# Two-map attention: value products in three rounded passes over pairs of query tiles

## What is computed

```python
def diff_attention(q, k, v, pos, slopes, lam):
    scale = A_HEAD_DIM ** -0.5
    ...
    s = jnp.einsum('bqhmd,bkhmd->bhmqk', qb, k).astype(jnp.float32) * scale
    ...
    s = s - slopes[None, :, None, None, None] * dist
    p = jax.nn.softmax(s, axis=-1)
    w = p[:, :, 0] - lam * p[:, :, 1]
    return jnp.einsum('bhqk,bkhe->bqhe', w.astype(v.dtype), v)
```

## Time and profile before

| what | us |
|---|---|
| runs | 3290.07, 3291.96, 3292.62; median 3291.96 |
| profiled execution: its own time | 3290.69 |
| its span | 3288.9 |
| PE busy / DVE busy / ACT busy / POOL busy | 3188.6 / 1707.1 / 1131.5 / 997.7 |
| window 1467.40 to 1547.35, one head: PE / DVE / ACT / POOL busy | 79.95 / 52.93 / 43.02 / 17.50 |
| window 1867.00 to 1947.00, last head and after: PE / DVE / ACT / POOL busy | 80.00 / 44.60 / 46.65 / 25.23 |

### The profile page before, as it was taken

How to read it: one execution, slowest core, us unless ns; L and a number is a source line. 1 busy time by engine, 2 the same in 40 slices (tenths; PEclk the granted TensorE clock), 3 DMA queues, 4 the chain that set the end, 5 groups by cost and what they waited for, 6 DMA issues and landing times.

```text
span 3288.9 us, 52109 instructions
## 1 busy us (share of the span) xinstructions
PE 3188.6 (97%) x20350; PEld 2839.4 (86%) x20350; DVE 1707.1 (52%) x2867; ACT 1131.5 (34%) x2189; POOL 997.7 (30%) x688
## 2 busy tenths in 40 slices
PE   8999999999999999999999999999999999799997
PEld 6677768788888888999899899999999999699997
DVE  5554556765554535666666632277677033522223
ACT  3433333333332214555555541166465111300002
POOL 3112224787773333222222132210000223022222
PEclk9999999999999999999999999999999999799998
DMA  4011112122225112000000012211111341478888
GB/s 160 26 33 33 33 65 103 64 77 78 77 82 207 52 45 98 20 20 20 20 21 26 14 43 79 74 43 48 38 45 50 129 156 51 181 257 315 307 315 291
DMA packets 94214, 312.01 MB, mean 95 GB/s; under 512 B 14690, under 2 KB 27810, under 8 KB 90832
## 3 DMA queue, kind: packets, MB, share of 16 engines
q1 hardware_dynamic: 68448, 248.16, 21.3%
q10 hardware_dynamic: 19424, 42.70, 3.4%
q0 software_dynamic: 6160, 18.63, 2.3%
HBM read 247.91 MB, written 56.22 MB: 92 GB/s over the span
## 4 chain that ended last, share of the span: by engine, by line
PE 54%; DVE 3%; DMA 1%; ACT 1%; issue 1%; POOL 0%; SPq 0%; ACTq 0%; POOLq 0%; DVEq 0%
PE PS L673 14%; PE PS L3162 7%; PE PS L3631 6%; PE PS L661 5%; PE PS L3226 4%; PE PS L3378 4%; PE PS L3193 3%; PE PS L3661 3%; PE PS L3412 3%; PE PS L3454 2%; DVE EB L2837 1%; PE PS L3227 0%; DMA fin<-h_rows 0%; PE PS L3175 0%; DMA h_rows<-y_row_b,pick_s_b 0%
## 5 line engine op out<-in xcount | busy, mean ns | idle before, releaser
L695 POOL CAST w_hi<-ring 128x1024 fp32r<-128x1024 f32 x130 | 138.1, 1062 | 1543.9 <-PE PS L673 401.4
L697 POOL TENSOR_TENSOR w_lo<-ring,w_hi 128x1024 fp32r<-128x1024 f32 x130 | 333.4, 2565 | 10.5
L2247 ACT ACTIVATE EA<-EA,small_sb 128x1040 f32<-128x1040 f32 x144 | 166.6, 1157 | 186.4 <-DVE small_sb L2690 186.3
L2690 DVE CUSTOM_DVE_ANT_0 EA<-PS,biasH,low_a 128x1024 f32<-128x1024 f32 x128 | 163.6, 1278 | 56.3 <-PE PS L3193 56.2
L3162 PE MATMUL PS<-u_hi,w_hi 128*128 128x348 f32 x504 | 173.5, 344 | 0.0
L3162 PE MATMUL PS<-u_lo,w_hi 128*128 128x348 f32 x504 | 162.1, 322 | 0.0
L3162 PE MATMUL PS<-u_hi,w_lo 128*128 128x348 f32 x504 | 161.8, 321 | 0.0
L1643 DVE TENSOR_TENSOR hid_lo<-hid,hid_hi 128x1024 fp32r<-128x1024 f32 x44 | 91.7, 2123 | 118.8 <-ACT hid_hi L1285 118.8
L1735 PE MATMUL PS<-u_hi,w_hi 128*128 128x512 f32 x352 | 146.8, 417 | 3.0 <-POOL w_lo L697 2.3
L1932 PE MATMUL PS<-t_hi,slot_hi 128*128 128x512 f32 x352 | 138.9, 395 | 5.9 <-DVE t_lo L1544 3.3
L3226 PE MATMUL PS<-Va,PTa 128*128 128x128 f32 (+1 forms) x1152 | 139.9, 275 | 0.0
(11 more groups left out here) (502 smaller groups left out, 8639.5 us busy)
## 6 DMA issues: line engine op xcount, KB each, us to landing
ring<-in_stream SPq DMA_DIRECT2D x130, 512.0 KB, 3.5
w_gate_sb<-in_w_gate SPq DMA_DIRECT2D x64, 512.0 KB, 6.8
w_up_sb<-in_w_up SPq DMA_DIRECT2D x64, 512.0 KB, 8.1
w_down_sb<-in_w_down SPq DMA_DIRECT2D x64, 512.0 KB
gu_raw<-in_gate_up SPq DMA_DIRECT2D x22, 1024.0 KB, 5.6
hid_keep<-hid_out SPq DMA_DIRECT2D x17, 512.0 KB, 2.9
hid<-hid_keep ACTq DMA_DIRECT2D x15, 512.0 KB, 16.4
x_keep<-xT ACTq DMA_DIRECT2D x1, 4176.0 KB, 13.8
```

The costliest lines, as they stand in the source:

```text
L695: pool.tensor_copy(w_hi[j][:, :, :], w_raw[j][:, :, :]).then_inc(S["w_rounded"], 1)
L697: pool.tensor_tensor(w_lo[j][:, :, :], w_raw[j][:, :, :], w_hi[j][:, :, :], ALU.subtract).then_inc(S["w_split"], 1)
L2247: act.activation(e[0:m, :], e[0:m, :], ACT.Exp, scale=-1.0, bias=small[0:m, 8 + 2 * par + k:9 + 2 * par + k], accum_out=small[0:m, 12 + 2 ...
L2690: dve.tensor_tensor_reduce(e[0:m, 0:T1], wide(2 * k, T1, m), bias, -1.0, low_a[0:m, t, k:k + 1], ALU.add, ALU.min, low).then_inc(S["aa_max ...
```

## The change

The value product is done for groups of tiles, (0,1), (2,3), (4,5), (6,7,8), with values stationary and probabilities moving (256 or 272 columns), in three passes of rounded operands; the results come out as columns, are copied to SBUF and turned back with transposes. ACT writes the turned probabilities rounded (PA_hi) in two copies of 512 columns and one for the meta rows; DVE writes the rest (PA_lo). The same holds for the values. Four of the nine tiles of o_tok (t = 5 to 8, HELD = 5) no longer stay in SBUF: their results go to small staging tiles and by DMA to `o_keep` in DRAM, four DMAs a head on ACT's queue, and are loaded back after the last head.

```diff
+A_GROUPS = ((0, 1), (2, 3), (4, 5), (6, 7, 8))
+HELD = 5
...
 POOL
                 for t in range(NT + 1):
+                    if t == HELD:
+                        pool.wait_ge(S["keep_ld"], 32 + 16 * SPILLED)
                     heads_norm(pool, t).then_inc(S["as_np"], 1)
                 split(pool, FIRST_BRANCH, 1, MG0 // 2 + 2, FIRST_BRANCH - 2)
...
 ACT, for each step t of a head
+                        if t % 2 and before:
+                            results(*before)
                         if after:
                             exp(after[0], (after[1] + after[2]) % 2, after[2], 0)
+                        if t % 2 == 0 and before:
+                            take_columns(*before)
+                        if t % 2 or t == NT:
+                            take_pt(h, t)
                         if after:
                             exp(after[0], (after[1] + after[2]) % 2, after[2], 1)
+                        if t % 2 == 0 and t < NT:
+                            take_pt(h, t)
+                        if t % 2 and before:
+                            squares(*before)
...
 ACT, after the last head
+                take_columns(HEADS - 1, NGA - 1)
                 sigmoid(0, 0, EARLY_GATES[0], 0)
+                results(HEADS - 1, NGA - 1)
+                squares(HEADS - 1, NGA - 1)
                 roots(slice(HEADS - 1, HEADS))
+                act.wait_ge(S["keep_st"], KEPT + 16 * SPILLED * HEADS)
+                for t in range(HELD, NT + 1):
+                    m = P if t < NT else META
+                    act.dma_start(o_tok[0:m, t, :], o_keep[0:m, t - HELD, :]).then_inc(S["keep_ld"], 16)
...
 DVE
+                def attend(h, par, t, fresh=False, lower=None, first=False):
                     scores(h, par, t, 0, fresh)
                     scores(h, par, t, 1, fresh)
+                    if lower and first:
+                        lower_probs(*lower)
                     combine(h, par, t, fresh)
+                    if lower and not first:
+                        lower_probs(*lower)
...
-                            attend(h, (odd + t + 1) % 2, t + 1, first)
+                            attend(h, (odd + t + 1) % 2, t + 1, first, (h, t), t % 2 == 1)
...
 PE
+                def values(h, g, half):
+                    n, w = 9 * h + A_GROUPS[g][-1], group_width(g)
+                    pe.wait_ge(S["probs_lo"], 3 * n + 2 + half)
+                    if g == 0:
+                        pe.wait_ge(S["values_lo"], 3 * h + 2 + half)
+                    for i in (range(4, NT + 1) if half else range(4)):
+                        v_hi, v_lo = (Va_hi[:, i, :], Va_lo[:, i, :]) if i < NT else (Vam_hi[:, :], Vam_lo[:, :])
+                        for k, (v, probs) in enumerate(((v_hi, PA_hi), (v_hi, PA_lo), (v_lo, PA_hi))):
+                            last = mm(bank(7, w), v, probs[:, i, 0:w], start=(i == 0 and k == 0), stop=(i == NT and k == 2))
+                    if half:
+                        last.then_inc(S["aa_o"], 1)
+                def turn_back(h, g, n):
+                    pe.wait_ge(S["columns_in"], NGA * h + g + 1)
+                    pe.wait_ge(S["probs_lo"], 3 * n + 1)
+                    for k, t in enumerate(A_GROUPS[g]):
+                        m = P if t < NT else META
+                        last = turn(bank(7, P, k * P, m), turned_back[:, k * P:k * P + m])
+                    last.then_inc(S["aa_v"], 1)
...
 PE, for each step t of a head, after scores(t+1)
+                        before = None if first and t == 0 or t == NT or t % 2 else group_before(h, t)
+                        if before:
+                            values(*before, 1)
                         unit(h + 1, 1 - odd, kind, c, 0)
                         turn_probs(h, (odd + t) % 2, t, first)
                         unit(h + 1, 1 - odd, kind, c, 1)
+                        if t in (1, 3, 5, NT):
+                            values(h, min(t // 2, NGA - 1), 0)
+                        if before:
+                            turn_back(*before, 9 * h + t)
+                        if t == 0:
                             turn_values(h)
```

More of the change, by code:

```diff
@@ L348, in build @@
         ka_lo[1] = o.put("ka_lo1", [P, TP], F32R)
+        kmeta = o.put("kmeta", [P, 2 * META])
+        Vam_hi, Vam_lo = (o.put(n, [P, P], F32R) for n in ("Vam_hi", "Vam_lo"))
+        stage = [o.put("stage0", [P, P])]
         tok_at = (top - 4 * (NT + 1) * D) // 32 * 32
@@ new lines, in take_pt @@
+                    if cols.start == 0 and n:
+                        act.wait_ge(S["aa_o"], NGA * h + t // 2)
+                    act.activation(PA_hi[0:META, NT, cols], bank(7, m, 3 * P, META), ACT.Copy).then_inc(S["aa_pt"], 1)
+                    for b in range(2):
+                        act.wait_ge(S["aa_t"], 3 * n + 2 + b)
+                        act.activation(PA_hi[:, 4 * b:4 * b + 4, cols], bank(5 + b).rearrange("p (j n) -> p j n", n=P)[:, :, 0:m], ACT.Copy).then_inc(S["aa_pt"], 1)
@@ new lines, in take_columns, with home, results @@
+                def take_columns(h, g):
+                    w = group_width(g)
+                    act.wait_ge(S["aa_o"], NGA * h + g + 1)
+                    act.activation(turned_back[:, 0:w], bank(7, w), ACT.Copy).then_inc(S["columns_in"], 1)
+                def home(h, t, m):
+                    return o_tok[0:m, t, bass.ds(h * P, P)] if t < HELD else stage[t - HELD][0:m, :]
+                def results(h, g):
+                    act.wait_ge(S["aa_v"], TURNED_A * h + 4 + g)
+                    if g == NGA - 1 and h + 1 < HEADS:
+                        act.wait_ge(S["values_lo"], 3 * (h + 1) + 1)
+                    for k, t in enumerate(A_GROUPS[g]):
+                        m = P if t < NT else META
+                        if t == HELD:
+                            act.wait_ge(S["keep_st"], KEPT + 16 * SPILLED * h)
+                        seen(act)
+                        act.activation(home(h, t, m), bank(7, P, k * P, m), ACT.Copy, scale=small[0:m, 48 + t:49 + t]).then_inc(S["aa_y"], 1)
@@ new lines, in squares @@
+                def squares(h, g):
+                    for t in A_GROUPS[g]:
+                        m = P if t < NT else META
+                        act.wait_ge(S["aa_y"], 9 * h + t + 1 + CREDIT)
+                        if t >= HELD:
+                            act.dma_start(o_keep[0:m, t - HELD, h * P:(h + 1) * P], stage[t - HELD][0:m, :]).then_inc(S["keep_st"], 16)
+                        act.activation(junk[0:m, :], home(h, t, m), ACT.Square, accum_out=ss2[0:m, t, bass.ds(h, 1)]).then_inc(S["aa_ssq"], 1)
+                        act.wait_ge(S["aa_ssq"], 9 * h + t + 1)
@@ L2721, in head @@
                         if t < NT:
-                            attend(h, (odd + t + 1) % 2, t + 1, first)
+                            attend(h, (odd + t + 1) % 2, t + 1, first, (h, t), t % 2 == 1)
                         elif not last:
-                            attend(h + 1, 1 - odd, 0)
+                            attend(h + 1, 1 - odd, 0, False, (h, t), True)
+                        else:
+                            lower_probs(h, t)
+                        if not last:
+                            kind, c = UNITS[t]
+                            if kind == "k":
+                                lower_keys(h + 1, 1 - odd, c, WEAVE)
+                            elif kind == "q":
+                                lower_queries(h + 1, c)
+                        if t == 0:
+                            lower_values(h)
                         if last:
@@ L2752, in _ @@
                 dve.wait_ge(S["as_r"], 2)
[L2753 removed]
+                for tiles, m in ((slice(0, 3), P), (slice(3, HELD), P), (slice(HELD, NT), P), (slice(NT, NT + 1), META)):
+                    if tiles.start == HELD:
+                        dve.wait_ge(S["keep_ld"], 32 + 16 * SPILLED)
                     last_head_norm(dve, tiles, m).then_inc(S["as_n"], 1)
@@ L3315, in drain @@
                     if c == KD - 1:
-                        values(h, 1, NT - 1, 18 * h + 2 * NT + 1)
+                        for half in range(2):
+                            values(h, NGA - 1, half)
                 pe.wait_ge(S["aa_max"], 18 * HEADS + CREDIT)
                 project_split(pe, 1, EARLY_GATES[0], *triple(0), drain)
-                pe.wait_ge(S["aa_y"], 9 * HEADS - 1 + CREDIT)
-                values(h, 1, NT, 18 * HEADS)
                 def turn_heads(t):
```

247 lines of the change are left out of this document (118 added, 129 removed).

## The result

| | us |
|---|---|
| changed kernel, four runs | 3315.28 to 3318.72, median 3316.98 |
| kernel before, four runs beside it | 3290.07 to 3293.60, median 3292.29 |
| ratio | 1.0076, 95% interval 1.0058 to 1.0093: slower by 0.76% |
| profiled execution: its own time, its span | 3318.04, 3316.2 |

The forecast was 3304 (3276 to 3321), slower. The direction and the range held; of the 24.7 us between the medians the forecast's sum had 12.

What follows compares the result with a forecast made beforehand. PE was taken to bound a loop head before, the latency chain the last head after. Terms -5 + 12 - 3 + 3 + 5 = +12 on 3290.69 give 3302.7, with 1.3 for the median 3304; range 3276 to 3321.

Steps and rivals of the forecast that it cites:

- Seven heads, -5: Loop heads: PE saves some 4.5 us a head, waits (a) to (d) take 3.75, 0.7 gained per head.
- (a): Step 3: POOL's split delays DVE's 16-column copy, so PE waits 1.1 us for the odd tile's first rounded rest.
- (b): t=6: POOL's halving of the bias lengthens combine by 1.1 in front of turn_back; costs 1.0 us a head.
- (c): Step 8: the short step 7, its split and DVE's queue make tile 8's rests late by 1.4 us.
- (d): t=0: turn_values waits for both halves of tile 0's rests, 0.25 us a head.
- It fits by 0.15: Plain even step: the meta part of lower_probs is done at 8.05, PE reaches turn_back at 8.20, so no wait.
- The last head, +12: The latency chain sets the pace; tile 1's to tile 8's scores on DVE take 56.7 us against 45.0.
- rival 3: PE's clock falls in the last head, granted clock under 0.8 over it; up to +17, to 3321; chance 0.08.
- After tile 8, +5: Fewer products behind tile 8 -3, ScalarE's chain before the first transposes +3, GpSimd's norms and split behind the reload +5.
- rival 1: DVE's room suffices, PE's saving comes through, waits under 1 us a head; -17, 3275; chance 0.22.
- rival 2: It cancels: half the waits reach PE, heads -18, last head +9, tail +8, 3291; chance 0.2.
- Rival 4: Products cost more than mixer B's pace, at 0.16 us each PE's gain is gone; 3316; chance 0.05.

Runs made afterwards that it cites:

- e2_turn_later: Changed kernel with the turn-backs of tile pairs (0,1), (2,3), (4,5) moved behind the next odd step's scores; median 3304.24 us, ratio to before 1.0040.
- e9b_f32_later: Changed kernel with later turn-backs and, in the last head alone, one float32 value product for three rounded ones, no subtraction; 3297.58 us, ratio to before 1.0021.
- e11_fill_full: Changed kernel with later turn-backs, plus four full-height products of zeros a step in the last head from its second step; 3303.97 us, ratio to before 1.0039.

## Why the prediction was right, and where it was off

**What PE pays.** The product price held where nothing stood in front: twelve of 256 columns in 1.42 to 1.43. In most places twelve took 1.5 to 1.6. PE's busy time of a head was summed to 75.5 and measured at 76.7 to 76.9. Two terms of that: fifteen products behind scores took 1.87 (1421.67 to 1423.54) instead of 1.79, and a turn-back of two tiles 0.34 (1428.60 to 1428.94) instead of 0.22. Taken over all six heads, from start to start, the new products and turn-backs are 15.1 a head where the sum had 14.04, and the 0.45 for halves of units behind the same operation did not come (36.3 against 36.2 for all of them); the old products, 18.7 instead of 18.09, gave 0.6 more back. PE's idle time was 3.4 against the 3.75 walked. VectorE rose to 64.6 and not to 68.1: its new subtractions are 14.5 a head, as summed within 0.7, but combine's last instruction became shorter (1791 to 1532 ns in the mean of 48).

**Seven heads, -5.** Measured +4.5 from the first halving to the last. This is the step that failed first. Six of them cost 1.0 each more than summed: 1.3 of PE's own time, less 0.3 of waits. The waits were right item by item: (a) 0.47 to 0.82 for 1.1, (b) 1.14 to 1.17 for 1.0, (c) 1.40 to 1.49 for 1.4, (d) none in these heads for 0.25. "It fits by 0.15" held too: the turn-backs of the plain even steps did not wait. The experiments bear this out: moving the turn-back gave back 1.18, which is (b), and the other form of the copy 1.91 of (a) and (c). The remaining miss is head 0: the wait (d) was 1.83 + 0.24 there, where the kernel before had 0.57, and the clock's fall behind it cost another 1.7, together the bulk of the 3.4 by which this head missed its -0.7.

**The last head, +12.** Measured +15.6, outside the bound of +13. The steps at full clock were close to the walk (8.39 and 8.57 for 8.3, 7.45 for 7.3, and 9.85 for the first step's 9.9 in e2_turn_later); the walk took 5.9 to combine's end where the earlier trace rows gave 6.22, and the step of 8.57 shows 6.0. Two falls of the clock to 0.83 to 0.85 added some 3 (10.06 against the like step's 8.57, and 11.19 against 9.85 for the first step of e2_turn_later, whose clock was 1.00). That was rival 3, which I had held to be a case of its own with the point at 0.8 over the whole last head. Over it the granted clock was 0.94: a rival does not have to win to cost something, and its small form belonged in the forecast's own term. "The latency chain sets the pace" was right, with one link more than its name says: the runs without subtraction, with later turn-backs and with float32 products show the order of the turn-back (3.2), then the forming of the rests and the three products in all steps (7.7 from e2_turn_later to e9b_f32_later, of which some 3.0 are clock falls, as e11_fill_full had 54.39 without them). That VectorE's subtractions are the larger part of the 4.6 left is argued, not shown.

**After tile 8, +5.** Measured +4.2, by other terms. The -3 for fewer products behind tile 8 came: from tile 8's reduction to the start of gate 1's tile 21.2 before, 18.4 after. From there to the first FIRST_BRANCH product it was 16.75 before and 23.70 after, +7.0 for the +8 summed. The +3 for ScalarE's chain came as 2.65 of idle time in front of the first transposes (the profile names no releaser; VectorE's norm of the first tiles, behind ScalarE's roots, ran from 1953.55), and the low clock behind it, which the sum had not, cost 1.6. The +5 for GpSimd's norms and split behind the landing is the term whose mechanism was wrong: they stood behind the landing as written, but TensorE did not wait for them. What it waited for was VectorE's order, 2.13, with the held tiles' norm in front of the low parts of the first tiles, which I had not priced. The landing came earlier than estimated (12.3 behind the start of gate 1's tile, not 14). The spill alone, on the kernel before, costs 5.1 by the same wait and the same fall of the clock.

**In-loop stores, nothing.** Right, by the kernel before with the spill: 79.94 a head with and without.

**Rivals.** Room on DVE (rival 1) and cancellation (rival 2) did not come: waits on PA_lo sum to 3.4 a head. Rival 4 fell with the product's price. The direction was right for the reason given in the last head, and in the loop the waits were the forecast ones; its size was half of what came, since the loop was taken as a gain and two falls of the clock and head 0 were not in it. That 3316.98 lies in the range is in part luck: it is outside the forecast's own 3295 to 3316, and only rival 3, held at 0.08 and not what happened as a whole, carried the range to 3321.

## What to carry to other kernels

An instruction that waits for the end of a latency chain must not stand in front of the work that starts the next chain: moving a 0.34 us transpose behind the next scores was worth more (1.18 us a head) than removing 8 us of VectorE's work a head (0.72). When a change takes an engine off its full load, small blockings of another engine that lay under it for nothing come to the surface: look them up before, and take them out with the change. A walk that takes each collision from a row can be right to some tenths even with fits of 0.15 us; what it missed here were things it had not walked: the first head, the engine's own small costs in front of each group of products, the clock, and a wait on a late DMA in front of work that does not need it.

## What the hardware showed that I had not expected

- Products of 64 rows and of 128 rows in turn start 0.35 us apart where those of 128 rows alone start 0.16 apart (348 columns, granted clock 1.00).
- The granted clock fell to 0.73 in a step in which TensorE was busy 12.60 of 12.6 us, if with these slow alternations; idle time of the engine, as the profile counts it, is not what all falls follow.
- A reduction over an axis of length 1 does a copy's work in the same 0.16 us, and was not held beside GpSimd in any of six heads (mean 163 ns in 96).
